# Sliding-span attention: one vector instruction for bias, scale, copy and row maximum, and a root multiplied into the queries by GpSimd

## The reference, cut to what matters

```python
def sliding_window_attention(q, k, v, sinks, rel_bias):   # cut
    s = einsum('bnqhgd,bnkhd->bnhgqk', qb, kb) * (HEAD_DIM ** -0.5)
    s = where(valid, s + bias, NEG_INF)              # bias: rel_bias[t5_bucket(dist)]
    p = softmax(concatenate([s, sink], axis=-1), axis=-1)[..., :-1]
    return einsum('bnhgqk,bnkhd->bnqhgd', p, vb)

def swa_branch(h, w_in, sinks, w_out, rel_bias):
    q, k, v, z = split(h @ w_in, ...)
    o = sliding_window_attention(q, k, v, sinks, rel_bias)
    return (o * silu(z)) @ w_out
```

## Time and profile before

| | |
|---|---|
| runs | 2065.87, 2066.5, 2066.71 us; median 2066.5 us |
| profiled execution | 2067.48 us, of which the span of the trace is 2065.7 us |
| mean granted clock of TensorE | 0.973 of full speed |
| PE busy | 1947.3 us, 94% of the span |
| DVE busy | 1324.2 us, 64% |
| ACT busy | 896.2 us, 43% |
| POOL busy | 517.5 us, 25% |
| `stage_swa`, first scores to the last PV product | 1364.5 to 1475.7 us |

### The profile page before, as it was taken

How to read it: one execution, slowest core, us unless ns; L and a number is a source line. 1 busy time by engine, 2 the same in 40 slices (tenths; PEclk the granted TensorE clock), 3 DMA queues, 4 the chain that set the end, 5 groups by cost and what they waited for, 6 DMA issues and landing times.

```text
span 2065.7 us, 25536 instructions
## 1 busy us (share of the span) xinstructions
PE 1947.3 (94%) x9856; PEld 1546.0 (75%) x9856; DVE 1324.2 (64%) x2035; ACT 896.2 (43%) x1430; POOL 517.5 (25%) x511
## 2 busy tenths in 40 slices
PE   7998888999999999999999999998989999989988
PEld 5786675888757888868888877777777766578867
DVE  7997875846729446456566844767557477738373
ACT  5445546411159313432242344435544555535332
POOL 0571110466238614024221611013101211100000
PEclk9999889999999999999999999999999999999999
DMA  4335331243422535625535925311133410023311
GB/s 161 98 133 156 114 111 56 84 153 137 136 82 92 163 107 160 213 62 156 190 95 151 209 88 126 88 62 42 52 102 93 127 41 31 31 82 122 102 62 62
DMA packets 71305, 223.70 MB, mean 108 GB/s; under 512 B 17153, under 2 KB 17841, under 8 KB 70161
## 3 DMA queue, kind: packets, MB, share of 16 engines
q1 hardware_dynamic: 43488, 159.40, 23.6%
q0 software_dynamic: 24240, 55.79, 9.8%
q10 hardware_dynamic: 3456, 6.87, 1.3%
HBM read 204.80 MB, written 14.81 MB: 106 GB/s over the span
## 4 chain that ended last, share of the span: by engine, by line
PE 68%; DVE 8%; ACT 5%; issue 3%; DVEq 0%; ACTq 0%
PE bank L486 19%; PE bank L487 19%; PE bank L488 19%; PE bank L485 2%; PE bank L3501 1%; ACT swa_s L3362 1%; PE bank L3469 1%; DVE ring_low L448 1%; ACT ring_high L443 1%; PE bank L621 1%; PE bank L2871 1%; DVE swa_s L3280 1%; PE bank L2160 1%; DVE lru_x L2074 1%; PE bank L3486 1%
## 5 line engine op out<-in xcount | busy, mean ns | idle before, releaser
L448 DVE TENSOR_TENSOR ring_low<-ring,ring_high 128x1024 fp32r<-128x1024 f32 x265 | 365.0, 1388 | 348.0 <-ACT ring_high L443 347.6
L486 PE MATMUL bank<-h_high,ring_high 128*128 128x512 f32 x1240 | 504.7, 407 | 36.4 <-DVE h_low L1542 12.1
L443 ACT ACTIVATE ring_high<-ring 128x1024 fp32r<-128x1024 f32 x283 | 297.1, 1056 | 541.0 <-PE bank L488 534.8
L487 PE MATMUL bank<-h_low,ring_high 128*128 128x512 f32 x1240 | 491.7, 396 | 0.0
L488 PE MATMUL bank<-h_high,ring_low 128*128 128x512 f32 x1240 | 491.0, 396 | 0.0
L486 PEld LDWEIGHTS bank<-h_high,ring_high 128*128 128x128 f32 x1240 | 238.4, 192 | 102.7 <-issue 41.6
L487 PEld LDWEIGHTS bank<-h_low,ring_high 128*128 128x128 f32 x1240 | 238.5, 192 | 52.8 <-issue 4.3
L488 PEld LDWEIGHTS bank<-h_high,ring_low 128*128 128x128 f32 x1240 | 238.2, 192 | 51.2
L448 POOL TENSOR_TENSOR ring_low<-ring,ring_high 128x1024 fp32r<-128x1024 f32 x18 | 53.7, 2984 | 287.0 <-ACT ring_high L443 287.0
L486 PE MATMUL bank<-gated_high,ring_high 128*128 128x512 f32 x192 | 76.5, 399 | 1.4 <-DVE gated_low L3079 1.1
L488 PE MATMUL bank<-gated_high,ring_low 128*128 128x512 f32 x192 | 74.8, 390 | 0.0
(11 more groups left out here) (553 smaller groups left out, 3918.4 us busy)
## 6 DMA issues: line engine op xcount, KB each, us to landing
ring<-slabs SPq DMA_DIRECT2D x292, 512.0 KB, 3.3
acs_rows<-acs_rows POOLq DMA_DIRECT2D x16, 512.0 KB, 4.2
s_outputs<-s_ca POOLq DMA_DIRECT2D x4, 1152.0 KB, 6.7
x<-xT SPq DMA_DIRECT2D x2, 2048.0 KB, 7.7
exp_acs<-acs_rows POOLq DMA_DIRECT2D x16, 256.0 KB, 9.2
s_b<-s_br POOLq DMA_DIRECT2D x8, 512.0 KB, 4.2
s_rows<-s_powers POOLq DMA_DIRECT2D x16, 256.0 KB, 7.0
s_inputs<-s_w POOLq DMA_DIRECT2D x8, 512.0 KB, 4.1
```

The costliest lines, as they stand in the source:

```text
L443: act.activation(self.ring_high[:, self.splits_before[s] % AHEAD, :], self.ring[:, s % RING, :], ACT.Copy)\
L448: dve.tensor_tensor(self.ring_low[:, s % RING, :], self.ring[:, s % RING, :], self.ring_high[:, self.splits_before[s] % AHEAD, :].bitcast( ...
L486: pe.matmul(out, w[0], x[0], start=start, stop=False)
L487: pe.matmul(out, w[0], x[1], start=False, stop=False)
```

## The change

The eight instructions at L3280 become `tensor_tensor_reduce`, which writes out (scores + bias) * -0.125 and gives, for each row, the minimum of what it wrote. So `L.S` holds the negated logits, and the row minimum is the negated row maximum. The two reductions and one small operation go; a scalar_tensor_tensor forms the minimum of the negated sink and that value, and the exponential takes scale=-1. The bias table is laid out eight times larger (ACT copy with scale=8.0), so that the factor 1/8 covers scores and bias. The per-token factor can no longer ride on L3280: POOL multiplies each of the eight tiles of `L.Q` in place by the root during the stage for K, and PE waits for tile j before its scores. `C.st[:, 1]` is no longer made by `token_root_on_dve`.

```diff
@@ Entry.token_root_on_dve
-        C.vchain.link(dve, dve.reciprocal(C.st[:, 0, 0:TC], C.st[:, 0, 0:TC]))
-        dve.tensor_scalar(C.st[:, 1, 0:TC], C.st[:, 0, 0:TC], 64 ** -0.5, None, ALU.mult).then_inc(self.by_token.sem, 1)
+        dve.reciprocal(C.st[:, 0, 0:TC], C.st[:, 0, 0:TC]).then_inc(self.by_token.sem, 1)
@@ swa_bias, copy
-        act.activation(L.BV[:], C.bank[u.b][0:16, 0:384], ACT.Copy).then_inc(C.bank_read[u.b], 1)
+        act.activation(L.BV[:], C.bank[u.b][0:16, 0:384], ACT.Copy, scale=8.0).then_inc(C.bank_read[u.b], 1)
@@ stage_swa, scores(j) on PE
+                pe.wait_ge(L.q_rooted.sem, L.q_rooted.at(j))
@@ stage_swa, logits(j) on DVE
-                        ins = dve.scalar_tensor_tensor(
+                        ins = dve.tensor_tensor_reduce(
                             out=L.S[:, j % 2, n, e, lo:256], in0=C.bank[u.b][:, n % 2 * 256 + lo:n % 2 * 256 + 256],
-                            scalar=C.st[:, 1, n:n + 1], in1=L.BT[:, j + 8 * e, lo:256], op0=ALU.mult, op1=ALU.add)
+                            in1=L.BT[:, j + 8 * e, lo:256], scale=-0.125, scalar=LARGEST, op0=ALU.add, op1=ALU.min,
+                            accum_out=st[:, 0, n, e:e + 1])
+                        if n % 2 == 0:
+                            ins.then_inc(first.sem, 1)
...
-                ln(dve.tensor_reduce(st[:, 0, 0, :], L.S[:, j % 2, 0, :, P:256], AX.X, ALU.max))
-                ln(dve.tensor_reduce(st[:, 0, 1:4, :], L.S[:, j % 2, 1:4], AX.X, ALU.max))
+                dve.wait_ge(first.sem, first.at(TC * j + TC - 1))
                 sink = C.col("sinks", 0, 16)[:, j::8].unsqueeze(1).to_broadcast([P, TC, 2])
-                ln(dve.tensor_tensor(st[:, 0], st[:, 0], sink, ALU.max))
-                ln(dve.tensor_tensor(st[:, 1], sink, st[:, 0], ALU.subtract))
-                dve.tensor_scalar(st[:, 0], st[:, 0], -1.0, None, ALU.mult).then_inc(mx.sem, 1)
+                ln(dve.scalar_tensor_tensor(out=st[:, 0], in0=sink, scalar=-1.0, in1=st[:, 0], op0=ALU.mult, op1=ALU.min))
+                dve.tensor_tensor(st[:, 1], sink, st[:, 0], ALU.add).then_inc(mx.sem, 1)
@@ before logits(0)
-            L.entry.token_root(dve, 0)
@@ exps(j) on ACT
-                        ins = act.activation(s, s, ACT.Exp, bias=st[:, 0, n, e:e + 1], accum_out=st[:, 2, n, e:e + 1])
+                        ins = act.activation(s, s, ACT.Exp, scale=-1.0, bias=st[:, 0, n, e:e + 1], accum_out=st[:, 2, n, e:e + 1])
@@ branch_swa
-    stage_entry(C, entry, KD, copy_to(L.Q))
-    L.k_tile = stage_gemm(C, 1, hk, entry.times_root(L.K), "vector")[0][0]
+    q_tiles = stage_entry(C, entry, KD, copy_to(L.Q))
+    L.q_rooted = C.reserve("swa_q_rooted", KD)
+
+    def root_queries(pool):
+        pool.wait_ge(entry.rooted.sem, entry.rooted.at(0))
+        for j, (u, _) in enumerate(q_tiles):
+            C.read(pool, u)
+            pool.tensor_tensor(L.Q[:, j, :], L.Q[:, j, :], entry.root, ALU.mult).then_inc(L.q_rooted.sem, 1)
+    L.k_tile = stage_gemm(C, 1, hk, entry.times_root(L.K), "vector", side=Side(pool=root_queries))[0][0]
```

More of the change, by code:

```diff
@@ L42 @@
 C_GATE = C_Q + DM
+LARGEST = 3.0e38
 NEG = -1e30
@@ L1613, in token_root_on_dve @@
         C.read(dve, u)
-        C.vchain.link(dve, dve.reciprocal(C.st[:, 0, 0:TC], C.st[:, 0, 0:TC]))
-        dve.tensor_scalar(C.st[:, 1, 0:TC], C.st[:, 0, 0:TC], 64 ** -0.5, None, ALU.mult)            .then_inc(self.by_token.sem, 1)
+        dve.reciprocal(C.st[:, 0, 0:TC], C.st[:, 0, 0:TC]).then_inc(self.by_token.sem, 1)
     def token_root(self, eng, t):
@@ L3212, in stage_swa @@
     mx, ex, pn = C.reserve("mx", NJ), C.reserve("ex", NJ), C.reserve("pn", NJ)
-    zr = C.reserve("swaz", 1)
+    zr, first = C.reserve("swaz", 1), C.reserve("swa_first", TC * NJ)
     gate = L.gate
```

## The result

The changed kernel takes 2078.69 us (median of four runs, 2075.87 to 2079.97); the kernel before, run beside it, 2066.61 us (2065.87 to 2069.48). The ratio is 1.0054, with a 95% interval of 1.0037 to 1.0071: slower by 0.5%, where 2057.3 us and "faster" were forecast. The time lies outside the range. The profiled execution took 2079.86 us with a span of 2078.1, against 2067.48 and 2065.7 before.

What follows compares the result with a forecast made beforehand. A loop of waits through the maximum, 13.47 us, was taken to bind; then 12.02 us would. Last probabilities 9.2 us earlier: 2067.48 less 9.2 is 2058.3, less 1.0 for the median 2057.3 us; range 2054 to 2064.5.

Steps and rivals of the forecast that it cites:

- Loop A: Cycle through the row maximum on DVE and ACT: binds at 13.47 us, loses 1.98, becomes 11.49 (10.53 to 13.13).
- the new block: DVE's eight new instructions with reads, plus two small operations: 3.93 us (2.97 to 5.57), against 5.91 before.
- rival 3: The new vector instruction streams at half rate: from no change to 9 us slower, 2075.5 us; chance 0.08.
- rival 1: The new instruction's accumulator read is dear, up to 0.19 us each: 2059.5 to 2064.5 us in all; chance 0.17.
- The products on POOL: Eight query-tile products during K's stage, at most 16.7 us, done by 1366.2, hidden: cost nothing.
- Loop B: Gate-input cycle from PE's fourth bank of scores through z and DVE back: 12.02 us, slack 1.44, binding next.
- Evacuation, gate factor and low part follow at 0.60 each: DVE's three operations from reading z in the gate-input cycle: 1.81 us together.
- rival 2: PE's granted clock still dips, once or twice, 1.6 to 3.2 us worse: 2059 to 2060.5 us; chance 0.10.

Runs made afterwards that it cites:

- e1: Changed kernel, but POOL waits for step j's probabilities before making the low part of that step's slab: 2053.65 us, ratio 0.9932.
- e4: Kernel before with only POOL's query products, PE's wait for them and the constant 0.125: 2067.39 us (2061.42 to 2082.05), ratio 1.0007.
- e7: Changed kernel with POOL's split waiting for the probabilities, plus a useless 896-column DVE reduction before the low part from j = 2: 2066.94 us, ratio 0.9996.
- e9: Changed kernel, unaltered, run again on another chip: 2075.98 us against 2066.48, ratio 1.0043.

## Why the prediction was wrong, point by point

*Loop A and the new block: right in mechanism, cautious in size.* It was priced at 3.93 us. From the first L3281 at 1448.09 to the end of L3293 (1451.20 and 0.17) it is 3.28 us, 0.65 below the forecast and inside its bounds. The eight with their reads take 2.68 us of it, for 3.42. The accumulator read is an instruction of its own, 83 ns, but it lies under the next main part, and between two of them it costs nothing. Half rate (rival 3) is out: 420 - 288 = 132 ns for 128 columns, 1.03 ns a column as before. The dear read (rival 1) is out too. The first interval shows it, 10.75 us for 13.46.

*The products on POOL: right.* They ran from 1334.56 to 1351.28 (the last one starts at 1349.44 and takes 1.84), and the first scores began at 1364.3 behind V.

*Loop B binds next: right, and its terms were not.* The step that failed is "Evacuation, gate factor and low part follow at 0.60 each": the low part was priced as if nothing could hold DVE off. With it failed the 6.82 us ahead of it, which takes a full clock for granted. Fourth bank to fourth bank in the changed kernel, 1413.10 to 1430.47:

- fourth bank to z's evacuation: 10.01 us (1413.10 to 1423.11), for 6.82: matmuls at half the clock, +3.2;
- evacuation, factor and low part: 3.99 us (to 1427.10), for 1.81: the collision, +2.2;
- probabilities: 2.63 us (to 1429.73), for 2.65;
- gated output to the fourth bank: 0.74 us, as forecast.

In sum 17.37 for 12.02. In e1, with both terms put right by one wait, the period is 12.02 to 12.03.

Added up over the stage: the fourth banks were forecast at 1412.4, 1424.4, 1436.4 and 1448.5, and came at 1413.10, 1430.47, 1447.89 and 1465.11. The last probabilities were forecast at 1457.1 and came at 1478.91: 21.8 us late, of which 0.7 were there at the first of these banks, 15.9 came in the three periods and 5.2 behind the last bank. That is 12.6 us later than before (1466.35). The prediction let what stands behind them keep its length, and it did not: to the end of the last PV product it takes 6.5 us, where it took 9.3 before. So the stage ends only some 10 us later.

*The clock, rival 2, was named, and its condition came out the other way.* It was to fade as waits shrank to 0.5 us; they grew to 2.3. Its price, 1.6 us once or twice, was taken from a dip that lay in part under the slack of loop A. Here the loop that binds has PE in it, so slower matmuls lengthen loop B by their whole amount. They don't lengthen the wait: PE's own work grows by as much (17.37 - 15.09 = 2.28, and at the full clock 12.02 + 2.2 less 11.9 = 2.3). What renews the wait in each step is the collision. The clock costs 3.2 us in each of three periods and 3.0 behind the last fourth bank. The prediction gave "slower" a chance of 0.06, all of it for the half rate of rival 3, and its five chances add up to 1.00, with nothing for what it had not seen. That POOL may slow DVE it said once, of the eight products in the stage for K; no rival of it has POOL's slab splits holding DVE off in this stage.

*What should have been seen.* The collision is in the trace before, with the roles reversed, in rows of POOL that were not read because POOL looked idle. They are from POOL's timeline there, with DVE's row behind:

```profile
1375.48 2.40 POOL L448 TENSOR_TENSOR ring_low<-ring,ring_high 128x1024 fp32r<-128x1024 f32 x1 [70.32 <-ACT ring_high L443]
...
1453.88 3.96 POOL L448 TENSOR_TENSOR ring_low<-ring,ring_high 128x1024 fp32r<-128x1024 f32 x1 [9.50 <-ACT ring_high L443]
```

```profile
1453.32 2.29 DVE L3300 TENSOR_TENSOR swa_s<-swa_s,swa_st 128x2048 f32<-128x2048 f32 x1
```

The same split takes 2.40 us beside reductions of DVE, and 3.96 when DVE's multiply began 0.56 us before it; the multiply loses nothing. The 1.6 us more are nearly the 1.7 that were left of the multiply. POOL had the time, so nobody paid. The prediction moved ACT's exponentials earlier and never asked what else on ACT moves with them: the slab split behind them (L443) became released by PE instead of by the end of the exponentials, and POOL's split with it, onto DVE's low part.

The Trainium skill (SBUF — State Buffer, Who interferes with whom) states this as an exclusive lock: a VectorE instruction with two SBUF inputs and a GpSimd instruction that reads SBUF share ports, the one that is issued first keeps them for its whole length, and the other blocks entirely. The traces agree: by 0.55 us one way (POOL 3.95, DVE 2.29) and by 0.06 us the other (POOL 2.36, DVE 4.45). It also says that a VectorE instruction with at most one SBUF input, outside the modes that use both ports, does not contend. The trace of e1 agrees: POOL's split starts 0.16 us into L3315, which reads a bank and one SBUF operand, and keeps its 2.36 us; and the L3281 that starts at 1421.96, in the middle of the split, takes 0.29 us as elsewhere. This rule, put beside the order of ACT's queue, would have warned of a DVE loss of up to the 2.4 us of the split in the path that was about to bind; with the 2.2 us measured, 12.02 + 2.2 is 14.2 us, worse than the old 13.46 before any fall of the clock.

*Left open:* what decides whether and how soon the clock falls behind a wait of 1.2 to 2.3 us; the 2.5 us of the span outside the stage; the long runs of e4.

## What to carry to other kernels

Before an instruction becomes earlier, follow everything behind it in its queue: what it releases may land beside something else, and two engines released by the same event can meet in the same way in every step, as here. An instruction of an idle engine that has two durations in the trace is the warning, for when the roles turn the busy engine pays; making the idle engine wait cured it here. And where TensorE sits inside the loop that binds, price a wait with the slower matmuls behind it, not by its own length.

## What the runs showed of the hardware that was not expected

- Which of two engines starts first decides which pays, and a lead of 60 to 80 ns was enough: 2.86 for 0.68 us (128x512) and 4.45 for 2.29 (128x2048) on DVE with POOL 0.07 and 0.06 us ahead, 1.92 for 0.17 (128x8) with POOL 0.46 ahead; 3.96 for 2.40 on POOL with DVE 0.56 ahead.
- The fused add, scale, minimum and copy from a PSUM bank takes 420 ns for 256 float32 columns and 288 for 128; its accumulator read is a row of 83 ns under the next instruction.
- Of two equal waits of PE of 1.22 us, 13.2 us apart in e7, one left the granted clock at 1.00 and one was followed by 0.79. Behind waits of 2.3 us the period had 0.80 in the changed kernel, and once 0.89 in e9.
